# State-space stage: the first pair's read-out taken twice, from the two rotated products

## The chip, the core and the metric

The kernel runs on one core of a Trainium2 chip. The time is the device time of one execution in microseconds. The engines named here are TensorE (matrix products and transposes, into PSUM banks), VectorE and ScalarE (element-wise work), GpSimd, and SyncE, which issues most of the DMA transfers.

## The reference

Two transformer-like blocks of two layers each, on 256 tokens of width 1024. The change lies in one mixer of the second block, a diagonal state-space layer in 64 groups of 16 channels with 64 complex states each. Cut to what matters:

```python
def s5_mixer(h, lam, log_dt, b, c, d_skip, w_glu):
    a_bar = exp(lam * dt)                       # complex, one per group and state
    bu = einsum('gpi,lbgi->lbgp', b_bar, u)     # inputs into the states
    hs = scan: hs[t] = a_bar * hs[t-1] + bu[t]  # complex recurrence over 256 steps
    y = einsum('gop,lbgp->lbgo', cmat, hs).real # read-out
    y = y + d_skip * u
    g = gelu(y)
    val, gate = split(g @ w_glu)
    return val * sigmoid(gate)
```

After it come the residual sum and an MLP of width 4096 with squared ReLU.

## The kernel before

**How it is staged.** The kernel is one hand-ordered program. Each engine has its own instruction list, and semaphores join them; PSUM banks are planned by `Units`. Dense layers run as three products of a high and a low part of weights and activations (L732 to L734); ScalarE makes the high part (L1332) and VectorE the low one (L1723), as weights arrive by DMA into `ring`. The state-space stage lies between the two MLPs, at about 606 to 640 us.

**The state-space stage.** Time is cut into 32 chunks of 8 steps (`L = 8`, `NC = 32`). Inside a chunk the result is a product with precomputed taps (`tap_product`, L1189 to L1199); between chunks a state is carried. The 64 x 64 complex states are in 128 partitions (64 states of two halves, `GH = 2`) times 32 groups. `inject_product` (L1170 to L1178) makes the chunks' inputs to the states in four banks. VectorE turns them with `spin_pair` (L1806 to L1836), once for each pair of banks. It multiplies by cosines and sines of the state's angle (L1815, L1816) into `spun` and `crossed`, sums them into `driven` (L1820, L1821), runs the decay over the chunks with two scans (L1824) into `faded`, turns back with two more products (L1828, L1829), and sums or subtracts these into `states`, shifted by one chunk (L1834), with real and imaginary part side by side. Pair 0 does L1828 to L1834 in one piece of four; pair 1 does it in two.

TensorE then reads out. `read_out` (L1203 to L1216) multiplies each 64 x 32 block of states with 64 x 128 read-out weights into `state_out` banks, adding to what the taps left there. Part 0 uses the states of pair 0, part 1 those of pair 1. Each matrix product in float32 shows as two records. Loop L1235 to L1254 sets TensorE's order: taps of the part, then `keep_busy` (constant products into a bank that nobody reads, counts in `KEEP`, L46), then a wait for `states_ready`, then the read-out; part 1 waits twice, once for each half of its states. `weights_here` waits for the read-out's weights, which SyncE brings in four pieces a part (L670).

**Behind it.** ScalarE copies the `state_out` banks 0, 1 and 3 (L1628) and VectorE bank 2 (L2339, behind one low part of weights, L1723). TensorE transposes (`state_turn`, L1225), ScalarE applies the gelu (L1635 to L1645), and the gated linear unit's products (L732) follow.

**Storage.** `states` is `aux[:, 0:2048]`, pair 0 in its first half. `xg_at` holds the regrouped inputs of the chunks until TensorE has transposed them, and shares its place with `hT_hi`.

The program puts VectorE's order in the stage as: scale three chunk banks (L1804), clear the first column of `states` (L2334), `spin_pair(0)` with the fourth chunk bank scaled inside it after the first injection bank, `spin_pair(1)`, one low part of weights, the copy of bank 2.

## Time and profile before

| | us |
|---|---|
| median of 3 runs | 870.33 (870.22 to 870.56) |
| profiled execution | 871.13 |
| its span in the trace | 869.3 |
| TensorE busy | 852.5 (98%) |
| VectorE busy | 592.2 (68%) |
| ScalarE busy | 442.0 (51%) |
| mean granted clock of TensorE | 0.999 |

In the rows PE is TensorE, PEld its weight loads, DVE VectorE, ACT ScalarE, SP SyncE (SPq its queue of transfers). `L1828` is a line of the kernel. `out<-in` are the kernel's names of buffers, `x12` a count. In a timeline the first number is the start and the second the duration, and `[1.75 <-DVE aux L1834]` says that the engine stood idle for 1.75 us before, until that instruction released it. Matrix products overlap, so the start of the next group tells the pace better than a group's end.

### The profile page before, as it was taken

Reading aid. Unit: us, or ns where it says so; the run is one execution under the profiler, and the core shown is the slowest. Engines: PE = TensorE matmul, PEld = TensorE weight load, DVE = VectorE, ACT = ScalarE, POOL = GpSimd, SP = SyncE. Lnnn points to the kernel's source line nnn. Section 1 sums busy time; section 2 is a strip of 40 time slices with the busy share of each in tenths; the row PEclk is TensorE's granted clock in tenths of the full one; section 3 lists DMA queues with packets and bytes.
Section 4 is the critical chain, followed back from the end, with each engine's and each line's share of the span. In section 5 each row is a group of like instructions: output and inputs, shape, how many; then the busy total and the mean of one; then the engine's idle time right before and its main releaser. Section 6 shows DMA issues by size and latency. Waiting matters only on the chain.

```text
span 869.3 us, 13478 instructions
## 1 busy us (share of the span) xinstructions
PE 852.5 (98%) x5659; PEld 736.7 (85%) x5659; DVE 592.2 (68%) x738; ACT 442.0 (51%) x591; POOL 117.3 (13%) x74
## 2 busy tenths in 40 slices
PE   8999999999999999999999999999989999999998
PEld 7787888888788887888988889997868999999996
DVE  5694577756756678888798788786975655555553
ACT  5644465656954555753553436443254644444450
POOL 1000001111000004114054344440000000000000
PEclk9999999999999999999999999999999999999999
DMA  9936645555004537226455565556966465555521
GB/s 327 335 113 242 242 146 193 194 179 175 35 4 154 177 97 243 97 85 210 167 189 172 209 230 192 209 188 144 287 251 237 152 212 182 186 188 193 194 98 48
DMA packets 68117, 155.96 MB, mean 179 GB/s; under 512 B 3113, under 2 KB 6922, under 8 KB 68058
## 3 DMA queue, kind: packets, MB, share of 16 engines
q1 hardware_dynamic: 65024, 146.80, 50.0%
q0 software_dynamic: 2224, 7.67, 2.6%
q10 hardware_dynamic: 810, 0.63, 0.5%
q8 instruction: 45, 0.74, 0.3%
q14 instruction: 14, 0.11, 0.0%
HBM read 146.70 MB, written 7.34 MB: 177 GB/s over the span
## 4 chain that ended last, share of the span: by engine, by line
PE 88%; DVE 5%; ACT 2%; DMA 2%; SPq 1%; issue 1%; ACTq 0%; DVEq 0%
PE bank L732 18%; PE bank L733 18%; PE bank L734 18%; PE bank L1059 7%; PE bank L1061 7%; PE bank L1057 7%; PE bank L725 3%; DMA ring<-in_a_w_in 2%; PE bank L841 2%; PE bank L831 1%; PE bank L943 1%; PE bank L882 1%; DVE pT L1824 1%; PE bank L1131 1%; DVE wlo L1723 1%
## 5 line engine op out<-in xcount | busy, mean ns | idle before, releaser
L1723 DVE TENSOR_TENSOR wlo<-ring,whi 128x2048 fp32r<-128x2048 f32 (+1 forms) x103 | 251.6, 2449 | 136.8 <-ACT whi L1332 136.4
L1332 ACT ACTIVATE whi<-ring 128x2048 fp32r<-128x2048 f32 (+1 forms) x104 | 198.4, 1909 | 209.2 <-PE bank L734 144.1
L732 PE MATMUL bank<-whi,hT 128*128 128x512 f32 (+1 forms) x512 | 201.8, 394 | 5.3 <-DVE wlo L1952 1.9
L734 PE MATMUL bank<-whi,hT 128*128 128x512 f32 (+1 forms) x512 | 198.8, 388 | 0.0
L733 PE MATMUL bank<-wlo,hT 128*128 128x512 f32 (+1 forms) x512 | 198.7, 388 | 0.0
L1057 PE MATMUL bank<-hT,whi 128*128 128x256 f32 x512 | 145.3, 284 | 0.0
L1059 PE MATMUL bank<-hT,whi 128*128 128x256 f32 x512 | 144.9, 283 | 0.0
L1061 PE MATMUL bank<-hT,wlo 128*128 128x256 f32 x512 | 144.8, 283 | 0.0
L732 PEld LDWEIGHTS bank<-whi,hT 128*128 128x128 f32 x512 | 96.1, 188 | 27.8 <-issue 4.8
L734 PEld LDWEIGHTS bank<-whi,hT 128*128 128x128 f32 x512 | 96.1, 188 | 19.6
L733 PEld LDWEIGHTS bank<-wlo,hT 128*128 128x128 f32 x512 | 96.2, 188 | 18.9 <-issue 0.5
L1057 PEld LDWEIGHTS bank<-hT,whi 128*128 128x128 f32 x512 | 98.2, 192 | 0.6
L1059 PEld LDWEIGHTS bank<-hT,whi 128*128 128x128 f32 x512 | 98.2, 192 | 0.5
L1061 PEld LDWEIGHTS bank<-hT,wlo 128*128 128x128 f32 x512 | 98.2, 192 | 0.0
L732 PE MATMUL bank<-whi,hidT_hi 128*128 128x512 f32 x224 | 88.0, 393 | 0.0
L733 PE MATMUL bank<-wlo,hidT_hi 128*128 128x512 f32 x224 | 87.4, 390 | 0.0
L734 PE MATMUL bank<-whi,hidT_lo 128*128 128x512 f32 x224 | 87.2, 389 | 0.0
L1718 DVE SCALAR_TENSOR_TENSOR wlo<-ring,vcols,whi 128x512 fp32r<-128x512 f32 x64 | 43.8, 746 | 20.5 <-ACT whi L1328 20.5
L1328 ACT ACTIVATE whi<-ring,vcols 128x512 fp32r<-128x512 f32 x64 | 40.9, 711 | 19.2 <-PE bank L734 16.9
L732 PEld LDWEIGHTS bank<-whi,hidT_hi 128*128 128x128 f32 x224 | 42.1, 188 | 9.7 <-issue 1.2
L734 PEld LDWEIGHTS bank<-whi,hidT_lo 128*128 128x128 f32 x224 | 42.1, 188 | 8.9
L733 PEld LDWEIGHTS bank<-wlo,hidT_hi 128*128 128x128 f32 x224 | 42.1, 188 | 8.3
(296 smaller groups left out, 1027.6 us busy)
## 6 DMA issues: line engine op xcount, KB each, us to landing
ring<-in_w_ff SPq DMA_DIRECT2D x64, 1024.0 KB, 5.3
ring<-in_ple_gate_w SPq DMA_DIRECT2D x8, 1024.0 KB, 5.1
ring<-in_w_kv SPq DMA_DIRECT2D x8, 1024.0 KB, 5.0
ring<-in_b_w_in SPq DMA_DIRECT2D x8, 1024.0 KB, 5.0
ring<-in_a_w_in SPq DMA_DIRECT2D x7, 1024.0 KB, 14.5
ring<-in_w_in SPq DMA_DIRECT2D x6, 1024.0 KB, 5.6
ring<-in_w_glu SPq DMA_DIRECT2D x6, 1024.0 KB, 8.9
ring<-in_a_w_out SPq DMA_DIRECT2D x4, 1024.0 KB, 5.6
```

The lines of the kernel that those rows point to most:

```text
L725: last = pe.transpose(b[0:width, cc * S + t * P:cc * S + t * P + P], src[:, t, c * width:(c + 1) * width], ident)
L732: pe.matmul(bank_cols, high[:, at[0], at[1]], w_high, start=first, stop=False)
L733: pe.matmul(bank_cols, high[:, at[0], at[1]], w_low, start=False, stop=False)
L734: return pe.matmul(bank_cols, low[:, at[0], at[1]], w_high, start=False, stop=last)
L841: last = pe.matmul(b[:, :], pT[:, l, k, t * P:(t + 1) * P], ple_rows[:, k, nb * 512:(nb + 1) * 512], start=(k == 0), stop=(k == 1))
L1057: pe.matmul(b[:, at:at + S], w_high[:, kk, cols], hT_hi[:, k, :], start=k == 0 and at == 0, stop=False, skip_group_check=True)
L1059: pe.matmul(b[:, at:at + S], w_high[:, kk, cols], hT_lo[:, k, :], start=False, stop=False, skip_group_check=True)
L1061: last = pe.matmul(b[:, at:at + S], w_low[:, kk, cols], hT_hi[:, k, :], start=False, stop=k == KC - 1, skip_group_check=True)
L1328: ins = act.activation(whi[at][:, n], ring[:, slot[name], cols][:, n], ACT.Copy, scale=gain(gained[name[0]], 4 * (g % 2) + kk))
L1332: act.activation(whi[at], raw_rows(g), ACT.Copy).then_inc(high_made, 1)
L1718: ins = dve.scalar_tensor_tensor(out=wlo[at][:, n], in0=ring[:, slot[name], cols][:, n], scalar=gain(gained[name[0]], 4 * (g % 2) + kk), i ...
L1723: dve.tensor_tensor(wlo[at], raw_rows(g), whi[at], ALU.subtract).then_inc(low_made, 1)
```

## The change

`spin_pair(0)` no longer makes the states of pair 0. It writes the two products of the second turn, the cosine one and the sine one, each in the layout of states and shifted by one chunk, into two buffers `turned[0]` and `turned[1]` (the second with the minus sign folded into its real part), and TensorE reads out both with the same weights into the same banks. The counts of constant products in `KEEP` change from 12 and 5 to 2 and 3. `states_ready` is counted one further. Pair 1 stays.

```diff
--- before.py
+++ after.py
@@ -43,7 +43,7 @@
 LATE_TURN = 1
 REACH = 144
 WARM, HOLD = 9, 5
-KEEP = (0, 3, 12, 5)
+KEEP = (0, 3, 2, 3)
 
 SPLIT = ("u", "za", "a_out", "gate0", "k", "v", "q", "zb", "b_out", "gate1", "wc", "wq", "wk", "wv", "w_o",
          "val", "gate", "f1", "f2")
@@ -562,6 +562,7 @@
         states = aux[:, 0:2048].rearrange("p (x c) -> p x c", c=NC)
         spun, crossed, driven = (aux[:, 2240 + 1024 * n:3264 + 1024 * n].rearrange("p (r m c) -> p r m c", r=2, m=4)
                                  for n in range(3))
+        turned = [v.rearrange("p (x c) -> p x c", c=NC) for v in (aux[:, 0:1024], xg_at[:, 0:1024])]
         faded = pT[:, :, :, :].rearrange("p l k s -> p (l k s)").rearrange("p (r m c) -> p r m c", r=2, m=4)
         waves = h
         fades = sig[:, :, :].rearrange("p b (x c) -> p (b x) c", c=NC)
@@ -1200,6 +1201,21 @@
                                          start=(s == 0), stop=False, skip_group_check=True)
                 last.then_inc(pe_done, 1)
 
+            def read_out_turned(n):
+
+                wr = weights(("readout", 0), 32, P)
+                for half in range(GH):
+                    rows = slice(GP * half, GP * half + GP)
+                    for s in range(4):
+                        for r in range(2):
+                            for q in range(4):
+                                to = slice(32 * QS[q], 32 * QS[q] + 32)
+                                last = pe.matmul(bank(("state_out", half))[to, s * P:(s + 1) * P],
+                                                 turned[n][rows, 16 * r + 4 * q + s, :], wr[rows, 8 * q + 4 * r + s, :],
+                                                 start=False, stop=(n == 1 and r == 1), skip_group_check=True)
+                    if n == 1:
+                        last.then_inc(pe_done, 1)
+
             def read_out(part, halves, quarters):
 
                 wr = weights(("readout", part), 32, P)
@@ -1240,15 +1256,15 @@
                 if part == 0:
                     weights_here(("readout", 0))
                     keep_busy(KEEP[2])
-                    pe.wait_ge(states_ready, 1)
-                    for half in range(GH):
-                        read_out(0, (half,), range(4))
+                    for n in range(2):
+                        pe.wait_ge(states_ready, n + 1)
+                        read_out_turned(n)
                 else:
                     keep_busy(KEEP[3])
-                    pe.wait_ge(states_ready, 2)
+                    pe.wait_ge(states_ready, 3)
                     weights_here(("readout", 1), first=True)
                     read_out(1, (0, 1), (0, 1))
-                    pe.wait_ge(states_ready, 3)
+                    pe.wait_ge(states_ready, 4)
                     weights_here(("readout", 1))
                     read_out(1, (0, 1), (2, 3))
             for n in range(4):
@@ -1816,6 +1832,7 @@
                     dve.tensor_tensor(crossed[:, :, m], b[:, ::-1], both[1][:, :, m], ALU.mult).then_inc(dve_emptied, 1)
                     if pair == odd == 0:
                         scaled_chunks(3)
+                        dve.memset(turned[1][:, :, 0:1], 0.0)
                 dve.wait_ge(dve_emptied, u.emptied(("inject", 2 * pair + 1)))
                 dve.tensor_tensor(driven[:, 0], spun[:, 0], crossed[:, 0], ALU.add)
                 link(dve.tensor_tensor(driven[:, 1], spun[:, 1], crossed[:, 1], ALU.subtract))
@@ -1824,7 +1841,16 @@
                     ins = dve.tensor_tensor_scan(faded[:, r].rearrange("p m c -> p (m c)"), fade,
                                                  driven[:, r].rearrange("p m c -> p (m c)"), 0.0, ALU.mult, ALU.add)
                 link(ins)
-                for m in (slice(0, 2), slice(2, 4)) if pair else (slice(0, 4),):
+                if pair == 0:
+                    one, two = (v.rearrange("p r m (q c) -> p r (m q) c", c=NC)[:, :, :, 0:NC - 1] for v in (faded, faded[:, ::-1]))
+                    cos, sin = (v.rearrange("p r m (q c) -> p r (m q) c", c=NC)[:, :, :, 0:NC - 1] for v in both)
+                    to = [v.rearrange("p (r x) c -> p r x c", r=2)[:, :, :, 1:NC] for v in turned]
+                    dve.tensor_tensor(to[0], one, cos, ALU.mult).then_inc(states_ready, 1)
+                    dve.scalar_tensor_tensor(out=to[1][:, 0], in0=two[:, 0], scalar=-1.0, in1=sin[:, 0], op0=ALU.mult, op1=ALU.mult)
+                    dve.tensor_tensor(to[1][:, 1], two[:, 1], sin[:, 1], ALU.mult).then_inc(states_ready, 1)
+                    dve.wait_ge(states_ready, 2)
+                    return
+                for m in (slice(0, 2), slice(2, 4)):
                     dve.tensor_tensor(spun[:, :, m], faded[:, :, m], both[0][:, :, m], ALU.mult)
                     link(dve.tensor_tensor(crossed[:, :, m], faded[:, ::-1, m], both[1][:, :, m], ALU.mult))
                     for r, op in enumerate((ALU.subtract, ALU.add)):
@@ -1833,7 +1859,7 @@
                         to = states[:, 32 * pair:32 * pair + 32, :].rearrange("p (m r q) c -> p r m q c", m=4, r=2)[:, r, m, :, 1:NC]
                         ins = dve.tensor_tensor(to, one, two, op)
                     ins.then_inc(states_ready, 1)
-                    dve.wait_ge(states_ready, (2 if m.start == 0 else 3) if pair else 1)
+                    dve.wait_ge(states_ready, 3 if m.start == 0 else 4)
 
             def s5_powers():
 
```

## Rows read from the trace of the kernel before

**Rows 1.** The page, parts 1 and 4: busy time, and the chain that ended last.
```profile
PE 852.5 (98%) x5659; PEld 736.7 (85%) x5659; DVE 592.2 (68%) x738; ACT 442.0 (51%) x591; POOL 117.3 (13%) x74
...
PE 88%; DVE 5%; ACT 2%; DMA 2%; SPq 1%; issue 1%; ACTq 0%; DVEq 0%
```

**Rows 2.** Stretches: length, busy of PE, PEld, DVE, ACT, POOL; clock, DMA share, GB/s.
```profile
609.80:614.50 4.70, 4.70 (x142) 4.49 (x142) 3.04 (x7) 0.72 (x1) 0.00 (x0) 1.00 1.04 271
614.50:618.20 3.70, 3.70 (x126) 3.67 (x122) 3.63 (x5) 0.00 (x0) 0.00 (x0) 1.00 0.88 221
...
620.20:623.20 3.00, 2.95 (x13) 2.11 (x12) 2.93 (x5) 0.00 (x0) 0.00 (x0) 1.00 1.03 330
...
629.80:631.50 1.70, 0.00 (x0) 0.00 (x0) 1.65 (x4) 0.86 (x1) 0.00 (x0) 1.00 0.78 270
...
700.00:869.30 169.30, 165.47 (x1037) 150.00 (x1035) 85.93 (x62) 67.86 (x58) 0.00 (x0) 1.00 0.47 158
```

**Rows 3.** Timeline of TensorE through both read-outs, 620 to 636 us.
```profile
620.14 3.01 PE L1232 MATMUL bank<-hT 128*128 128x512 f32 x12
623.22 3.31 PE L1212 MATMUL bank<-ring,aux 64*32 64x128 f32 x128
626.46 1.96 PE L1198 MATMUL bank<-spare,work 128*32 128x128 f32 x64
628.34 1.45 PE L1232 MATMUL bank<-hT 128*128 128x512 f32 x5
631.54 1.95 PE L1212 MATMUL bank<-ring,aux 64*32 64x128 f32 x64 [1.75 <-DVE aux L1834]
633.64 1.95 PE L1212 MATMUL bank<-ring,aux 64*32 64x128 f32 x64 [0.15 <-DVE aux L1834]
```

**Rows 4.** Chain that ended last, 614 to 637 us: start, us, what.
```profile
614.48 0.69 DVE aux L1815
...
633.62 2.29 DVE wlo L1723
...
636.66 0.64 PE bank L1225 x4
```

**Rows 5.** Timeline of VectorE, 610 to 631 us.
```profile
610.83 0.11 DVE L2334 MEMSET aux<- 128x64 f32 x1
...
614.48 0.69 DVE L1815 TENSOR_TENSOR aux<-bank,h 128x512 f32<-128x512 f32 x1 [0.69 <-PE bank L1177]
...
619.51 1.23 DVE L1828 TENSOR_TENSOR aux<-pT,h 128x1024 f32<-128x1024 f32 x1
620.65 1.22 DVE L1829 TENSOR_TENSOR aux<-pT,h 128x1024 f32<-128x1024 f32 x1
621.90 0.67 DVE L1834 TENSOR_TENSOR aux<-aux 128x496 f32<-128x496 f32 x1
...
622.49 0.67 DVE L1834 TENSOR_TENSOR aux<-aux 128x496 f32<-128x496 f32 x1
623.19 0.69 DVE L1815 TENSOR_TENSOR aux<-bank,h 128x512 f32<-128x512 f32 x1
...
630.74 0.74 DVE L1834 TENSOR_TENSOR aux<-aux 128x248 f32<-128x248 f32 x2
```

**Rows 6.** Groups by line and shape on VectorE, whole span: busy, mean ns.
```profile
L1718 DVE SCALAR_TENSOR_TENSOR wlo<-ring,vcols,whi 128x512 fp32r<-128x512 f32 x64 | 43.8, 746 | 20.5 <-ACT whi L1328 20.5
...
L2082 DVE SCALAR_TENSOR_TENSOR aux<-bank,aux 128x384 f32<-128x384 f32 x16 | 8.1, 550 | 3.9 <-ACT aux L1478 3.9
```

**Rows 7.** Timeline of ScalarE: the work that waits behind the copies.
```profile
628.75 1.91 ACT L1332 ACTIVATE whi<-work 128x2048 fp32r<-128x2048 f32 x1 [1.56 <-DMA work<-in_w_glu]
```

**Rows 8.** SyncE's timeline, and the transfer issued last: size, us to landing.
```profile
624.34 2.13 SPq L670 DMA_DIRECT2D ring<-scratch_readout  x2
...
ring<-scratch_readout SPq DMA_DIRECT2D x1, 512.0 KB, 5.7
```

**Rows 9.** Who waited for whom from 640 us on: us, times, longest.
```profile
ACT whi L1332 <- PE bank L734: 57.8, 18, 3.5
```

## The prediction, made before any run of the changed kernel

> **What bounds the kernel now.** I read the page first. TensorE is busy for 98% of the span, and the chain that ended last lies on it for 88% and on VectorE for 5% [rows 1]. The share says only that TensorE is the usual bound; the change sits in a stage where it may not be. So next came the table of stretches from 609.8 us on, to find where TensorE stands still. From 629.80 to 631.50 us it has no work at all while VectorE is busy for 1.65 of 1.70 us, and in the stretches before it VectorE is as busy as TensorE (2.93 of 3.00 us) [rows 2]. TensorE's busy time there is not all useful either: 12 and 5 of its products (L1232) are constant products that `keep_busy` issues to no purpose of the result [rows 3]. The chain of waits settles it: from 614.5 us to the first transpose of the outputs at 636.66 us every piece of it is VectorE's or a hand-over [rows 4]. The timeline of VectorE gives its order and has no hole after the 0.69 us before 614.48 us [rows 5]. The stage is a VectorE chain with TensorE waiting behind it: 1.75 us before the first half of the second read-out (631.54 us), 0.15 us before the other half [rows 3].
>
> So time taken from VectorE between 614.48 and 633.62 us moves the end of the kernel, until something else is late.
>
> **What the change takes from VectorE.** For pair 0, before: two multiplications of 128x1024 (L1828, L1829) and two sums of 128x496 (L1834). They start at 619.51 us, and the next instruction, the first of pair 1, starts at 623.19 us [rows 5]: 3.68 us in all, by start times, which count overlaps and waits once.
>
> After: one multiplication of 2x16x31 = 992 elements a partition, one scalar_tensor_tensor of 496 (the sign of the sine product is folded into it) and one multiplication of 496.
> - The first: L1828 at 1024 elements lasts 1.23 us and its follower starts 1.14 us after it [rows 5]. From this L1828 to the two L1834 of 496 elements, 528 elements are worth 1.23 - 0.67 = 0.56 us, so 32 fewer are worth 0.03: 1.11 us.
> - The scalar_tensor_tensor: no row has it with this shape from the chip's own memory with a constant scalar. With a constant scalar, L2082 takes 550 ns at 384 elements; 112 more at the same slope are 0.12 us, so 0.67 us, what a 496-element sum takes. With a scalar read from memory, L1718 takes 746 ns at 512, so 0.73 at 496 [rows 6]. A follower starts about 0.08 us before the end in the first case (L1834: 621.90 to 622.49 is 0.59 us for a duration of 0.67 [rows 5]). So it is worth 0.59 to 0.65 us; I take 0.60, since the scalar here is a constant, as in L2082.
> - The last: 496 elements with the wait behind it, as the second L1834 from 622.49 to 623.19 us: 0.70 us [rows 5].
>
> Sum 1.11 + 0.60 + 0.70 = 2.41 us, against 3.68: **1.27 us less**, bounds 1.22 to 1.28. None of the access patterns is new: the 31-of-32 step stands in L1834, the exchanged halves and the repeated factors in L1828 and L1829, at the price of plain ones. For patterns merged in a new way I keep 0.1 us on either side.
>
> The added memset of 32 elements costs at most the 0.11 us of the one of 64 (L2334) [rows 5]. It stands behind the scaling of the last chunk bank, before the wait for the second injection bank, where VectorE is idle for 0.69 us before 614.48 [rows 5]: nothing. Behind it are the four injection multiplications of this bank; were the cover gone it would cost its 0.11 us. TensorE waits for the scaling, not for the memset.
>
> The Trainium skill has a rule that could be held against counting by instructions rather than elements ("VectorE: DVE Perf Modes", § The DRAIN you can't avoid): the next operation does not start before the pipe of the last one is empty. Here L1829 starts 1.14 us after L1828, which lasts 1.23 [rows 5], so start times are the better count. By full durations the sum would be 1.19 + 0.67 + 0.67 = 2.53 against 1.23 + 1.22 + 0.67 + 0.67 = 3.79, a gain of 1.26: the same.
>
> **What it adds to TensorE.** Before, the first read-out is 64 products in the program (128 records, since each float32 product shows twice) from 623.22 to the next group's start at 626.46: 3.24 us [rows 3]. After, it is taken twice: 6.48 us. Removed are 10 of the 12 and 2 of the 5 constant products. Twelve take 3.01 us with the last one's tail of about 0.4, so 0.23 each at start: 12 x 0.23 = 2.8 us is the pace, 10 of them 2.3 us, 2 more 0.46 us. TensorE thus gets 3.24 - 2.8 = 0.5 us more work, but it may start earlier: the first copy needs only the cosine product. Working forward:
> - taps end and the constant products start at 620.14; two of them: 620.60
> - cosine product ready at 619.51 + 1.2 = 620.7; with the 0.05 us from VectorE's end to TensorE's start, the read-out starts at 620.75
> - first copy to 623.99, second copy to 627.23. The second one's wait, for a product ready at 619.51 + 2.41 = 621.9, is long over
> - taps of the second part, 626.46 to 628.34 before [rows 3], so 1.88 us: to 629.11
> - three constant products, 0.7 us: 629.8
> - the first half of pair 1's states is ready at 631.5 - 1.27 = 630.2 (the sums of L1834 start at 630.74 and last 0.74 [rows 5]), so TensorE starts at 630.3
> - it takes 1.95 us with its tail [rows 3], to 632.2; the other half is ready at 633.6 - 1.27 = 632.3.
>
> So TensorE is ready 0.5 us before VectorE, where it was 1.75 before. **VectorE still sets the end of the stage**, and TensorE's 0.5 us more is hidden by that wait.
>
> Who else is moved? On TensorE's queue, behind the longer read-out, stand the taps of the second part, covered as worked out. ScalarE copies the first two outputs when they are done. It stands idle for 1.56 us before 628.75, where its next work waits for a transfer [rows 7]: the second copy ended at 627.19. It moves by the 0.77 us by which the read-out ends later (627.23 for 626.46), to 628.0, and still hides. No DMA is added or moved past another. The one transfer that comes close is the last piece of the second read-out's weights: SyncE issues the pair from 624.34 to 626.47 us, and the last takes 5.7 us [rows 8], so it lands at about 631.9 at the latest. TensorE wanted it at 633.64 and will want it at 632.3: 0.4 us to spare.
>
> **After the stage** the subtraction on VectorE (L1723, 633.62 [rows 4]), the copy, the transposes and the gelus follow one on another and start 1.27 us earlier as one. Then TensorE is busy for 165.47 of 169.30 us from 700 us on [rows 2], and from 640 us on the rounding of the weights on ScalarE (L1332) waits for TensorE 18 times, 57.8 us in all [rows 9], never long for a transfer: the weights are there early. Nothing there eats the gain.
>
> The profiled execution took 871.13 us (span 869.3, 1.8 around it), 0.8 above the median of 870.33. The sum is made against its own times: 871.13 - 1.27 = 869.86. The difference carries over: 870.33 - 1.27 = **869.1 us**, by the bounds and 0.1 for the patterns 868.9 to 869.3; 0.2 more on either side for hand-overs that settle otherwise gives 868.7 to 869.5. I call 0.2% (1.74 us) about what a measurement of this kernel can tell from no change; the gain is 0.15%.
>
> **The rivals.**
> (a) *TensorE becomes the bound.* Its margin is only 0.5 us. For: 32 products of the read-out show as 1.95 us a group in part 1, against 3.24/2 = 1.62 by pace in part 0 [rows 3]. If the four groups cost 1.95 each, they take 7.8 us, TensorE is ready at 631.1 instead of 629.8, 0.8 behind VectorE, and the second half starts at about 633.0: 0.7 of the gain is lost, 869.8 us. Against: 1.95 holds a tail that the next product would overlap, and the new loop walks one half at a time exactly as part 0's did. The Trainium skill ("TensorE: Matmul & The Clock Gate", § The mechanism of packing small matmuls) says that a weight load overlaps running matmuls only if it goes to other rows of the array. By that rule the new loop, which stays in one half of the rows, would be the bad order and part 1's, which changes halves, the good one. The rows say otherwise: 1.62 us a group for the bad order, 1.95 at most for the good one [rows 3].
> (b) *The clock falls, and the kernel is slower.* Constant products at full width are cut from 12 to 2 ahead of the read-out, and with them what keeps the array full. The granted clock is 1.00 in every stretch, the 2.4 GHz level [rows 2]. If it went to 1.2 GHz from the second copy (624.0 us) to the transposes, every TensorE piece doubles: +3.24 for the copy, +1.88 for the taps, +0.7 for the constant products, less 0.5 of margin, then +1.7 for each half of the second read-out: 5.3 + 3.4 = 8.7 us, 877.8 us. It decides once the loss passes 1.27 us of gain and 0.5 of margin, that is, from some 3.5 us of work at the lower level. Against: from 609.80 to 618.20 TensorE ran almost only narrow products (64 columns of weights) for over 8 us at 1.00 [rows 2], and the empty 1.7 us at 629.80 is nearly gone after.
> The same page (§ What's actually happening) says the clock is granted by how busy the engine has lately been; by that the changed kernel, with fewer holes, has nothing to fear, and the trace agrees as far as 1.00 goes.
> (c) *The last weights are late.* If its 0.4 us to spare is gone and the piece lands at 633.0 or later, the gain falls to 0.6 or less: 869.8 to 870.3 us. The row is one transfer in a full queue, and no row shows how such a one varies from run to run.
> (d) *More than the sum.* If VectorE's new products cost less than their elements say, or the gelu's hand-overs fall better, 0.5 us more: below 868.6.
>
> **How the numbers follow.** Forecast 0.70, (a) 0.12, (b) 0.06, (c) 0.06, (d) 0.06. Faster by over 0.2% is below 868.59 us: (d), 0.06. Slower by over 0.2% is above 872.07: (b), 0.06. The rest is within: 0.88. The range takes in the forecast and nearly all of (a) and (c): 868.6 to 870.3; it leaves out (b), (d) and the tails of (c), some 0.14.
>
> **What would show it.** Right: in the changed kernel the first instruction of pair 1 (L1815's kind) starts about 2.4 us after the scans end and not 3.7; the read-out of the first part stands as two runs of 3.2 us without a hole; TensorE waits for VectorE about 0.5 us before the next read-out; the first transposes start near 635.4 us; the clock stays 1.00. Wrong: a wait of VectorE's for nothing between scans and pair 1, TensorE without a wait at 630 us (then (a)), a wait for the weights of L670 (then (c)), a clock below 1.00 (then (b)), or a hole of over 0.3 us after 640 us that was not there before.

## The result: slower, because TensorE ran out of instructions and then lost its clock

| | us |
|---|---|
| kernel before, median of 11 executions | 870.52 (870.18 to 870.75) |
| changed kernel, median of 11 executions | 874.68 (870.31 to 876.09) |
| ratio, with 95% interval | 1.0043 (1.0034 to 1.0051) |
| profiled execution of the changed kernel, and its span | 872.81, 871.0 |

Forecast was 869.1 us, 868.6 to 870.3. The kernel is 4.2 us slower instead of 1.4 faster. Its executions also spread over 5.8 us where the old one's spread over 0.6; in the sessions of the experiments the old kernel itself spread over 1.6 to 3.4 us. The granted clock, a mean over the whole execution, is 0.993 to 0.998 in ten of them; the eleventh, the fastest at 870.31 us, has 0.999. The profiled execution, 872.81 us, is the second fastest of the eleven.

VectorE's timeline in the changed kernel (start, duration, line) answers to [rows 5]:

```profile
612.92 0.09 DVE L1835 MEMSET xg_at<- 128x32 f32 x1
613.63 0.69 DVE L1831 TENSOR_TENSOR aux<-bank,h 128x512 f32<-128x512 f32 x1 [0.62 <-PE bank L1178]
...
618.66 1.19 DVE L1848 TENSOR_TENSOR aux<-pT,h 128x992 f32<-128x992 f32 x1
619.77 0.67 DVE L1849 SCALAR_TENSOR_TENSOR xg_at<-pT,h 128x496 f32<-128x496 f32 x1
620.35 0.67 DVE L1850 TENSOR_TENSOR xg_at<-pT,h 128x496 f32<-128x496 f32 x1
621.05 0.69 DVE L1831 TENSOR_TENSOR aux<-bank,h 128x512 f32<-128x512 f32 x1
...
637.56 0.69 DVE L2365 COPY work<-bank 128x512 f32<-128x512 f32 x1 [3.30 <-PE bank L1228]
```

The new products take 2.39 us from 618.66 to 621.05; the sum said 2.41. The memset hides before the wait. But at the end of the stage VectorE now waits 3.30 us for TensorE. TensorE's timeline answers to [rows 3]:

```profile
619.20 0.73 PE L1248 MATMUL bank<-hT 128*128 128x512 f32 x2
619.90 3.30 PE L1213 MATMUL bank<-ring,aux 64*32 64x128 f32 x127
624.03 0.29 PE L1213 MATMUL bank<-ring,aux 64*32 64x128 f32 x1 [0.83 <-issue]
624.04 3.30 PE L1213 MATMUL bank<-ring,xg_at 64*32 64x128 f32 x127
629.13 0.29 PE L1213 MATMUL bank<-ring,xg_at 64*32 64x128 f32 x1 [1.79 <-issue]
629.37 3.51 PE L1199 MATMUL bank<-spare,work 128*32 128x128 f32 x64
632.81 1.03 PE L1248 MATMUL bank<-hT 128*128 128x512 f32 x3
633.77 3.76 PE L1228 MATMUL bank<-ring,aux 64*32 64x128 f32 x128
638.40 1.94 PE L1241 MATMUL bank<-cst,work 128*128 128x128 f32 x16 [0.86 <-DVE work L2365]
```

Two things are new. Before the last record of each copy of the read-out (a float32 product shows as two records) TensorE stands still for 0.83 and 1.79 us, and the reason is "issue": no wait that the profile shows. And behind the second hole the taps take 3.44 us to the next start where they took 1.88 [rows 3]. The table of stretches says why:

```profile
623.20:626.40 3.20, 2.37 (x102) 2.37 (x105) 3.13 (x5) 0.34 (x1) 0.00 (x0) 1.00 1.03 395
626.40:629.80 3.40, 1.61 (x48) 1.22 (x44) 3.30 (x6) 0.59 (x2) 0.00 (x0) 0.97 0.93 334
629.80:631.50 1.70, 1.70 (x40) 1.70 (x36) 1.62 (x4) 1.70 (x2) 0.00 (x0) 0.50 0.68 199
631.50:635.60 4.10, 4.10 (x97) 3.28 (x91) 2.29 (x1) 0.36 (x1) 0.00 (x0) 0.82 1.04 382
```

The clock (third number from the end) is 0.50, the 1.2 GHz level, where TensorE was empty before the change [rows 2]. In the chain that ended last VectorE's share falls from 5% [rows 1] to 3%:

```profile
PE 90%; DVE 3%; ACT 2%; DMA 2%; SPq 1%; issue 1%; ACTq 0%; DVEq 0%
```

**The account of this execution.** This stage began 0.85 us earlier than before, at 608.95 for the first injection product against 609.80 (the work ahead of it is the same; over all traces of this case the stage begins between 608.75 and 611.72 us), so all is counted from there. By the forecast the transposes should start at 636.66 - 0.85 - 1.27 = 634.54 us; they start at 638.40, 3.86 late. The start of the read-out, 619.90, is the forecast one. From there to the taps it took 9.47 us instead of 6.48, +2.99: the holes, 2.62, and about 0.2 after each until the products overlap again. Taps +1.56, constant products +0.26: 4.81 us, less the 0.5 of margin, so the second read-out starts 4.3 us late, at 633.77 for 629.45. It takes 3.76 us where the forecast had 3.95 with a wait for VectorE in it, and the hand-over behind it takes 0.86 for 1.07, since VectorE's weights no longer stand right before the copy: 3.9 us.

Against the kernel before, the stage of this execution is 2.6 us longer (29.45 us from the first injection product to the first transpose, for 26.86). The medians differ by 4.2 us. The other 1.6 us belong to slower executions of which there is no trace; nine of them are slower than this one, seven with a mean clock of 0.993 to 0.996 against 0.998 here. More time at the lower clock or longer holes would both explain them; neither is shown.

### The profile page after: what moved, and what is told of

It is laid out like the page before. It is cut to its first block, busy times and chain, and to the rows that moved or that the text cites. A ratio compares the mean times of both kernels' runs of the same rounds, so it can differ in the third digit from the quotient of the medians.

```text
span 871.0 us, 13710 instructions
## 1 busy us (share of the span) xinstructions
PE 854.7 (98%) x5775; PEld 739.5 (85%) x5775; DVE 590.8 (68%) x738; ACT 441.7 (51%) x591; POOL 117.2 (13%) x74
## 4 chain that ended last, share of the span: by engine, by line
PE 90%; DVE 3%; ACT 2%; DMA 2%; SPq 1%; issue 1%; ACTq 0%; DVEq 0%
PE bank L733 18%; PE bank L735 18%; PE bank L734 18%; PE bank L1060 7%; PE bank L1062 7%; PE bank L1058 7%; PE bank L726 3%; DMA ring<-in_a_w_in 2%; PE bank L842 2%; PE bank L1178 1%; PE bank L832 1%; PE bank L1213 1%; PE bank L1199 1%; PE bank L944 1%; PE bank L883 1%
```

## What the experiments asked

The holes are 128 records apart, each with a weight load of its own: 256 instructions. The page of the changed kernel counts its transfers of instructions:

```profile
q8 instruction: 46, 0.75, 0.4%
```

That is 16 KB each, over 13710 instructions of all engines. So **theory A**: TensorE's instructions arrive in blocks of 256; a read-out uses a block in 3.24 us [rows 3]; the next is not there in that time, since its transfer shares DMA engines that are full with data (share 1.03 and 0.93 above). The clock falls on top of it.

The Trainium skill ("Runtime: NRT & Kernel Launch", § Instruction fetch mechanics) states the same block, 16 KiB or 256 instructions, and that crossing one is mostly hidden. The trace agrees on the block; here the crossing was not hidden.

**Rival B**: the second copy is simply too much work, or too slow with its new buffers. **Rival C**: the holes alone, or the cut of the constant products alone, bring down the clock.

Where an experiment's time is compared, the median of the kernel before is that of the same chip session: 870.97 us for e1 to e4, 870.57 for e5, e6, e8 and e9, 871.14 for e7, e10 and e11, 870.80 for e12. The runs e3, e6, e7 and e10 leave out part of the result or make it from old data.

The medians hold noise that does not come from this stage. A cleaner measure is the length of the stage in each run's trace, from the first injection product to the first transpose of the outputs. Behind it every trace takes the same 232.6 to 232.8 us to its end. These are single executions:

| run | stage begins | transposes begin | stage, us | against before |
|---|---|---|---|---|
| before | 609.80 | 636.66 | 26.86 | |
| changed | 608.95 | 638.40 | 29.45 | +2.59 |
| e1, constant products back at 12 and 5 | 611.36 | 644.09 | 32.73 | +5.87 |
| e2, six products between the copies | 609.57 | 639.36 | 29.79 | +2.93 |
| e3, VectorE's side alone | 609.08 | 634.66 | 25.58 | -1.28 |
| e4, TensorE's side alone | 609.28 | 643.09 | 33.81 | +6.95 |
| e5, before with 2 and 3 constant products | 609.19 | 636.09 | 26.90 | +0.04 |
| e6, changed with light transfers | 609.60 | 635.30 | 25.70 | -1.16 |
| e7, changed with one light transfer | 609.15 | 637.24 | 28.09 | +1.23 |
| e8, GpSimd makes both sums | 609.42 | 635.00 | 25.58 | -1.28 |
| e9, GpSimd makes one sum | 609.82 | 637.22 | 27.40 | +0.54 |
| e10, before with light transfers | 611.72 | 638.60 | 26.88 | +0.02 |
| e11, e8 with 12 and 5 | 609.89 | 637.04 | 27.15 | +0.29 |
| e12, e8 with 17 and 4 | 608.75 | 634.84 | 26.09 | -0.77 |

The mean clock of a whole execution has to be read with the same care. In the traces of e1 and e10 the clock was also at 0.50 for some 3.4 us from about 35 us on, far ahead of this stage, and e10's mean is 0.998 although its stage ran at 1.00. So a mean of 0.998 alone does not place a fall here.

### e3: VectorE's side alone

```diff
-                    for n in range(2):
-                        pe.wait_ge(states_ready, n + 1)
-                        read_out_turned(n)
+                    pe.wait_ge(states_ready, 1)
+                    read_out_turned(0)
```
and `KEEP = (0, 3, 12, 5)`; the stop flags and the count that frees the banks move to this one copy.

> The changed kernel with the second copy of the read-out left out on TensorE (the sine product is made but never read out, so the first pair's part of the result is incomplete), and the constant products at 12 and 5. VectorE's side of the change stands alone. If the sum of the prediction for VectorE was right and everything lost is lost on TensorE, no hole is left and the time is 869.1 us (1.2 to 1.3 us under the kernel before). If VectorE's new products or what follows them cost more than thought, it is 870.3 us or more.

869.57 us, ratio 0.9988 (0.9979 to 0.9996). TensorE's timeline, from before the taps:

```profile
616.06 2.00 PE L1178 MATMUL bank<-work 128*64 128x32 f32 x62 [0.37 <-issue]
...
619.88 3.35 PE L1247 MATMUL bank<-hT 128*128 128x512 f32 x12
623.15 3.31 PE L1213 MATMUL bank<-ring,aux 64*32 64x128 f32 x128
626.39 1.96 PE L1199 MATMUL bank<-spare,work 128*32 128x128 f32 x64
628.28 1.43 PE L1247 MATMUL bank<-hT 128*128 128x512 f32 x5
629.64 3.96 PE L1227 MATMUL bank<-ring,aux 64*32 64x128 f32 x128
634.66 1.94 PE L1240 MATMUL bank<-cst,work 128*128 128x128 f32 x16 [1.07 <-DVE work L2363]
```

No hole in the read-outs. The gain, 1.4 us by medians and 0.35 to 1.8 by the interval, holds the 1.27 of the sum, and the stage of the trace is 1.28 us shorter. So VectorE's part of the forecast stands, and everything is lost on TensorE. A small hole of 0.37 us stands among the injection products, in e4 too, and in e5 one of 0.65: the shortage can show outside the read-outs.

### e4: TensorE's side alone

```diff
-KEEP = (0, 3, 12, 5)
+KEEP = (0, 3, 2, 3)
...
+                    for half in range(GH):
+                        read_out_idle(half)
                     for half in range(GH):
                         read_out(0, (half,), range(4))
```
`read_out_idle` is the same loop into the banks of the injections, which nobody reads by then.

> The kernel before with VectorE untouched, but with an extra copy of the first read-out on TensorE, into banks nobody reads, ahead of the real one, and the constant products at 2 and 3. TensorE's side of the change stands alone. The copies start at 623.2 instead of 620.7 us, so even without holes TensorE is some 0.8 us late for the second read-out: 871.3 us. Theory A (short of instructions): the same two holes, 256 instructions apart, and the clock falls behind them in most executions: 874 to 878 us. Rival (the holes come from the new buffers, or from the two copies adding into the same banks): no hole, 871.3 us.

876.74 us, ratio 1.0068 (1.0056 to 1.0081), with the old buffers, the old sums and separate banks:

```profile
622.70 3.60 PE L1226 MATMUL bank<-ring,aux 64*32 64x128 f32 x128 [1.84 <-DVE aux L1848]
626.02 3.30 PE L1212 MATMUL bank<-ring,aux 64*32 64x128 f32 x127
633.30 0.42 PE L1212 MATMUL bank<-ring,aux 64*32 64x128 f32 x1 [3.98 <-issue]
633.65 3.64 PE L1198 MATMUL bank<-spare,work 128*32 128x128 f32 x64
```

The hole stands at the same record of the second copy, 3.98 us long. At the first copy's border there is at most 0.3 us (3.60 for 3.30): TensorE had waited 1.84 us for VectorE before it, time in which a block could arrive. The new buffers and the adding into one bank are out. The theory said two holes; there was one large and one nearly closed.

### e6 and e10: fewer bytes in the way

```diff
-                sp.dma_start(val_rows[:, half, :].rearrange("p (k n) -> p k n", k=KC // 2),
+                many = 4 if half else 1
+                sp.dma_start(val_rows[:, half, 0:512 * many].rearrange("p (k n) -> p k n", k=many),
...
-                        sp.dma_start(ring[:, slot[name], at:at + 1024], src).then_inc(block_landed[slot[name]][q % 2], 16)
+                        wide = 128 if name[1] else 1024
+                        sp.dma_start(ring[:, slot[name], at:at + wide], src[:, 0:wide]).then_inc(block_landed[slot[name]][q % 2], 16)
```

> The changed kernel with two groups of transfers made small: the first half of the gated unit's value weights (a quarter of its bytes) and the weights of the second read-out (an eighth), so that part of the result is made from what lay there before. TensorE's and VectorE's lists are untouched. If the holes are instructions that come late because their transfer queues with the data on the DMA engines, they shrink to under half, the clock is 1.00 and the time 869 to 870.5 us. If they have a cause of their own on TensorE, they stay at 0.8 and 1.8 us or more, and the time at about 875 us.

869.72 us, ratio 0.9994 (0.9985 to 1.0002), clock 0.998 to 1.000:

```profile
624.16 0.29 PE L1215 MATMUL bank<-ring,aux 64*32 64x128 f32 x1 [0.27 <-issue]
624.17 3.30 PE L1215 MATMUL bank<-ring,xg_at 64*32 64x128 f32 x127
627.89 0.29 PE L1215 MATMUL bank<-ring,xg_at 64*32 64x128 f32 x1 [0.42 <-issue]
```

With TensorE's and VectorE's lists untouched the holes shrink from 0.83 and 1.79 to 0.27 and 0.42 us, and the median is 5.0 us under the changed kernel's, each in its own session. This is the strongest evidence for theory A: nothing but bytes was taken away. By the queue of instruction transfers, in windows of 0.1 us, the blocks begin to move at 616.5, 621.3, 626.7 and 633.0 us in the changed kernel, 4.8 to 6.3 us apart; with light transfers at 617.7, 621.8 and 625.3, 4.1 and 3.5 apart.

The start of a block and the end of a hole belong together in every trace. There are sixteen holes of 0.25 us or more in this stage with "issue" as the reason, in ten of the runs, and TensorE goes on 2.2 to 2.8 us after a block has begun to move in all of them. What varies is the time before that: from TensorE's going on at such a border to the start of the next block it is 1.2 and 2.1 us in e6 and 1.3 to 6.0 us elsewhere. So of the time that a block takes, the part that gets longer is its wait to be moved.

The control is the kernel before with the same transfers made light:

> The kernel before with the same transfers made small as in e6_light_transfers (same parts of the result left to old data). It is the control: its time says what light transfers give without the change. If instructions are never short in the kernel before, 870.3 to 870.6 us, nothing gained, and the changed kernel's 869.72 us with light transfers is a gain of 0.6 to 0.9 us of the 1.27 that the sum gave. If it drops to about 869.7 too, the change gains nothing even without holes.

870.79 us, ratio 0.9996 (0.9987 to 1.0005): nothing gained that can be measured. So light transfers help the changed kernel alone. What the change is worth in that pair of kernels the times can't tell: by medians about 0.5 us (870.79 - 869.72 = 1.07, of which 0.57 is the difference between the two sessions' kernel before), but the two ratios are 0.9994 and 0.9996 and neither interval excludes 1. The traces say more: the stage is 1.16 us shorter in e6 and as long as before in e10, with 0.7 us of holes left.

### e7: which transfer

Of the edit of e6 only the first part, the value weights.

> The changed kernel with only the first half of the gated unit's value weights made small (a quarter of its bytes; part of the result is made from what lay there before); the second read-out's weights are whole again. It stands in the queue between the pieces of the second read-out, from 622 us on. If this transfer holds up the block of instructions behind the second hole, that hole shrinks to under 1 us and the first (0.8 us, before this transfer is issued) stays: 870.5 to 872 us. If the read-out weights are what holds it up, the hole stays at 1.8 us or more: 874 to 875 us.

873.43 us, ratio 1.0026 (1.0012 to 1.0040). In the profiled execution the holes are 1.05 and 1.52 us. That misses both sides of the expectation, but lies nearer to the second: together the holes are as long as in the changed kernel, 2.57 us for 2.62. By the difference to e6 the read-out's own weights are the larger part of what stands in the way; no run has these alone made light. Of its 12 executions, the five with a clock of 1.000 took 871.8 to 873.7 us; of the seven others, 0.992 to 0.999, one took 879.1.

### e1 and e2: constant products put back, or put between

```diff
-KEEP = (0, 3, 2, 3)
+KEEP = (0, 3, 12, 5)
```

> The changed kernel with the counts of constant products put back from 2 and 3 to 12 and 5, and nothing else. The trace of the changed kernel shows two holes of TensorE without any wait, 0.83 and 1.79 us, 256 instructions apart (issue), and a clock of 0.50 right behind the second. Theory A (TensorE runs out of instructions: they come in blocks, and the products of the read-out use them up faster than they come; the hole then drops the clock, because full-width products no longer surround it): the clock is back at 1.00 or nearly, the constant products stand where TensorE waited for instructions, and the time is 870 to 871.5 us. Theory B (TensorE's added work alone makes it late; the constant products do not matter for the clock): 2.8 us of constant products come on top of a TensorE that is already late, so about 877 us with the clock still at 0.996. Theory C (holes alone drop the clock, whatever stands around them): 874 to 876 us, as the changed kernel.

876.76 us, ratio 1.0067 (1.0053 to 1.0082):

```profile
624.83 2.98 PE L1213 MATMUL bank<-ring,aux 64*32 64x128 f32 x116
...
627.90 2.73 PE L1213 MATMUL bank<-ring,xg_at 64*32 64x128 f32 x105
633.46 1.06 PE L1213 MATMUL bank<-ring,xg_at 64*32 64x128 f32 x11 [2.83 <-issue]
634.45 3.64 PE L1199 MATMUL bank<-spare,work 128*32 128x128 f32 x64
```

Time and clock are those that rival B expected: once TensorE is the bound, constant products cost their full time. The hole B can't explain, and its place speaks for theory A. Ten more constant products ahead of the copies are 20 more instructions, and the hole stands before the eleventh record from the end instead of before the last: ten records with their loads, 20 instructions earlier. The border belongs to the instruction list, not to the work. The first border, now eleven records before the end of the first copy, shows no hole: the constant products put off the copies until 624.83 us, and the block for it began to move at 624.3. The one hole that is left is longer, 2.83 us. The clock falls all the same, to 0.50 from 632.4 us on, still within the hole (in e4 too, at 632.2). So what theory A said of the clock, that full-width products around the hole would hold it, is wrong.

e2 puts six products between the copies:

```diff
                         pe.wait_ge(states_ready, n + 1)
+                        if n:
+                            keep_busy(6)
                         read_out_turned(n)
```

> The changed kernel with 6 constant products (1.4 us at full clock) added between the two copies of the read-out. Theory A (short of instructions): these products take 12 instructions for 1.4 us, so they fill time in which TensorE would have stood still; the second hole shrinks from 1.79 us to about 0.4, TensorE ends the second copy no later than before, the clock stays at 1.00, and the time falls from 874.7 to 870 to 871.5 us. Theory B (TensorE simply has too much work): 1.4 us more, 876 us or more.

875.75 us, ratio 1.0056 (1.0038 to 1.0074). The hole did not shrink, it is 2.20 us long, and it moved seven records earlier for six products and a wait:

```profile
625.16 1.66 PE L1248 MATMUL bank<-hT 128*128 128x512 f32 x6
626.75 3.09 PE L1213 MATMUL bank<-ring,xg_at 64*32 64x128 f32 x120
632.05 0.42 PE L1213 MATMUL bank<-ring,xg_at 64*32 64x128 f32 x8 [2.20 <-issue]
```

The block behind it began to move at 629.7 us, 7.4 after the one before (622.3); in the changed kernel it was 5.4. So a block has no fixed time, and filling time ahead of it did not help. I had taken it as fixed. That it depends on the data in the queues when it is asked for fits e6, but is not shown for this block. The clock stayed at 1.00 in the profiled execution with 3.3 us of holes, so the holes are not an effect of a low clock. The two executions at 1.000 took 873.7 and 873.8 us, the four with a lower mean clock 875.3 to 878.9: without a fall the holes and the added products cost about 3 us against the kernel before, and the executions with a lower clock 1.6 to 5.1 more.

### e5: the constant products alone

The kernel before with `KEEP = (0, 3, 2, 3)`.

> The kernel before with only the counts of constant products changed, from 12 and 5 to 2 and 3. TensorE then waits idle for VectorE from about 620.6 to 623.2 us. If the cut of the constant products alone brings the clock down, the granted clock is under 1.00 in most executions and the time 873 us or more. If it takes the holes of instruction supply as well (theory A), the clock stays at 1.00 and the time is that of the kernel before, 870.3 to 871.2 us; the read-out may even start a block of instructions earlier, but TensorE waits for VectorE anyway.

870.77 us, ratio 1.0006 (0.9997 to 1.0015), but with a clock of 0.993 to 0.998 in all 11 executions. The stretches of the profiled one, with the wait of 1.56 us for VectorE in the first:

```profile
620.20:622.60 2.40, 0.84 (x10) 0.37 (x2) 2.33 (x4) 0.00 (x0) 0.00 (x0) 1.00 1.02 329
622.60:627.46 4.86, 4.86 (x128) 4.47 (x128) 4.79 (x7) 0.60 (x1) 0.00 (x0) 0.65 1.02 365
627.46:631.90 4.44, 4.44 (x71) 3.44 (x67) 4.33 (x8) 2.51 (x2) 0.00 (x0) 0.61 0.92 333
```

In the kernel before's own 33 executions of that session the mean clock is 0.998 in three and 0.999 or 1.000 in the others. The cut of the constant products is enough to lose the clock, without a second copy and without a hole in the read-outs; the hole of 0.65 us among the injections ended at 616.45 us, 7.7 us before the fall, and e3 kept 1.00 with one of 0.37 there. The time hardly shows the fall. The read-out takes 4.85 us instead of 3.24 and the taps 3.55 instead of 1.88, but behind them stood the 1.75 us in which TensorE waited for VectorE [rows 3], and the second read-out then passes in one piece of 3.31 us where its two halves with their wait took 4.05. The expectation that tied a falling clock to 873 us or more had forgotten that cover. The changed kernel has used it up.

### e8, e9, e11, e12: the same relief without TensorE

If the fault is instructions, VectorE should be relieved by an engine that isn't TensorE. GpSimd is idle here and takes over the sums of pair 0, with 17 and 3 constant products (`state_sum` is the sum of L1834 as a function of the engine):

```diff
+            pool.wait_ge(turns_made, 1)
+            for r in range(2):
+                ins = state_sum(pool, 0, r, slice(0, 4), *first_turns)
+            ins.then_inc(sums_made, 1)
...
+                if pair == 0:
+                    dve.tensor_tensor(first_turns[0], faded, both[0], ALU.mult)
+                    ins = dve.tensor_tensor(first_turns[1], faded[:, ::-1], both[1], ALU.mult)
+                    ins.then_inc(turns_made, 1)
+                    dve.wait_ge(turns_made, 1)
+                    return
```

> The kernel before with the same 1.27 us taken from VectorE in another way that adds no instruction to TensorE: GpSimd, idle here, makes the two sums of the first pair's states (from products in a buffer of their own), VectorE goes straight on to pair 1, and the constant products are 17 and 3. GpSimd took 3.0 us for 1152 elements in this kernel, so 2.6 us for 992: the first read-out starts at 624.6 instead of 623.2 us, its end and the taps of part 1 at 629.7, and the states of part 1 are ready at 630.3. If nothing but instruction supply spoiled the change, no hole appears and the time is 1.0 to 1.3 us below the kernel before, 869.2 to 870.0 us. If VectorE is slowed while GpSimd works (its L1723 took 2.63 instead of 2.29 us on average near GpSimd's work), some 0.4 us of it are lost; if GpSimd takes over 3.5 us, TensorE is late and the gain is gone.

869.88 us against 870.57, but the ratio is 0.9997 (0.9989 to 1.0006). The mechanism works: GpSimd takes 2.48 us for both, VectorE goes on at once and keeps its pace, TensorE has no hole in this execution:

```profile
621.58 2.48 POOL L574 TENSOR_TENSOR aux<-xg_at 128x496 f32<-128x496 f32 x2 [16.25 <-DVE xg_at L1839]
```
```profile
624.11 3.31 PE L1222 MATMUL bank<-ring,aux 64*32 64x128 f32 x128 [0.39 <-POOL aux L574]
...
635.00 1.94 PE L1235 MATMUL bank<-cst,work 128*128 128x128 f32 x16 [1.07 <-DVE work L2355]
```

The stage of this execution is 1.28 us shorter, all of VectorE's gain, but the executions run from 868.95 to 872.40 us. With one of the two sums on GpSimd (e9, `KEEP` 13 and 4) there are holes again:

> As e8_gpsimd_sums, but GpSimd makes one of the two sums and VectorE the other; constant products 13 and 4. VectorE is 0.6 us shorter instead of 1.27, and the first read-out waits for GpSimd only until about 623.4 us. If instruction supply and GpSimd's speed both leave room: 0.5 to 0.6 us below the kernel before. If GpSimd's time is the problem of e8, this one is the better of the two.

870.43 us, ratio 0.9997 (0.9984 to 1.0009), 0.65 and 1.57 us of holes in the profiled execution:

```profile
634.15 2.20 PE L1222 MATMUL bank<-ring,aux 64*32 64x128 f32 x82 [1.57 <-issue]
```

e11 leaves the counts at 12 and 5, e12 takes 17 and 4:

> The kernel of e8_gpsimd_sums with the constant products left at 12 and 5. TensorE has an empty 1.5 us before the first read-out (622.6 to 624.1) and is ready for the second one 0.4 us after VectorE's states instead of 0.1. If only VectorE's time counts: 0.3 us over e8, 870.2 us. If the clock needs the constant products right up to the read-out, it falls in some executions and the time spreads to 872 us and more.

> The kernel of e8_gpsimd_sums with 17 and 4 constant products instead of 17 and 3, to see whether this way to relieve VectorE beats the kernel before by more than the measurement's spread. The fourth product of the second group costs 0.23 us of TensorE's time, in which it is ready about 0.1 us after VectorE's states. If the gain of VectorE's 1.27 us holds: 869.7 to 870.2 us, 0.5 us or more below the kernel before measured beside it. If late instructions eat it in some executions, as in the kernel with one sum on GpSimd, the executions spread up to 872 us and the gain is not measurable.

e11: 870.77 us, ratio 0.9989 (0.9978 to 1.0000), spread 868.87 to 872.76, three of 12 executions at clock 0.996 and 872.6 to 872.8 us. e12: 870.28 us, ratio 0.9999 (0.9988 to 1.0010), spread 869.29 to 874.23. All medians lie 0.1 to 0.7 us under the kernel before, and no interval excludes no change. The traces of e8 and e12 show that 1.28 and 0.77 us can be had in the stage. Those of e9 and e11 show them lost, to the holes above and in e11 to one of 0.25 us and a wait of 0.60 for the read-out's weights. How often each happens no run tells, and part of the spread is noise that the old kernel has as well. None of the four is shown to beat the kernel before.

## Why the prediction was wrong, point by point

**VectorE's sum: right.** 2.39 us in the changed kernel and 2.40 in e3, forecast 2.41. Small terms too: the scalar_tensor_tensor is worth 0.58 us by start times, I took 0.60; the memset 0.09, hidden.

**Working forward on TensorE: the step that failed.** "First copy to 623.99, second copy to 627.23": the start was right, and so was the pace while there were instructions (127 records in 3.30 us with the tail, as 128 in 3.31 before [rows 3]). What was wrong is that a pace read from one group of 3.24 us [rows 3] was laid twice end to end. The group before it is 12 constant products, 24 instructions in 2.8 us; two copies are 512 instructions in 6.5. In the old program blocks of instructions began to move at 617.3, 622.5 and 628.6 us, 5.2 and 6.1 apart, and none was late; the new one uses a block up in 3.2 us while they begin to move 4.8 to 6.3 apart. The two copies measured 9.47 us instead of 6.48. Nothing in my sum counted instructions per microsecond, though the page lists their transfers and [rows 2] shows the DMA engines at 0.9 to 1.0.

**"TensorE gets 0.5 us more work": misleading.** It is right in time of products, and hides that 24 instructions (12 products with their weight loads) were exchanged for 256.

**Rival (a)**, TensorE becomes the bound, happened, but by holes and not by a slower pace, and at 3.0 us instead of the 1.3 that it priced; so its 869.8 us was far too low.

**Rival (b)**, the clock falls, happened too and was given 0.06. The argument against it, that narrow products had run for 8 us at 1.00, was a bad neighbour: e5 shows a fall with the fewer constant products and no second copy. Its price was fair in kind (taps 3.44 us for 1.88, as doubled) and too long in reach: in the profiled execution the clock is back at 1.00 by the second read-out. The sentence from the Trainium skill that the clock follows how busy the engine was ("TensorE: Matmul & The Clock Gate", § What's actually happening) I read as speaking for the change, as it would have fewer holes. The trace agrees as far as the changed kernel had more holes, not fewer, and its clock fell 0.5 us behind the longer one. But e2 kept 1.00 in its trace with longer holes and e5 fell with none in the read-outs, so how long TensorE stood still does not by itself tell the clock here.

**Rival (c)**, late weights, did not happen here. It did in e11, where TensorE waited 0.60 us for them before the last half. **(d)** did not.

**Behind the stage** nothing ate anything, as said: from 700 us on TensorE is busy for 167.15 of 171.00 us, and from the first transpose to the end it is 232.6 us in both kernels.

**What stays open.** Why blocks begin to move 3.5 us apart once and 7.4 another time: e6 and e7 together say that the read-out's weights count for more than the value weights, not by what rule. And what exactly drops the clock: e5 fell with a wait of 1.56 us and no hole in the read-outs, e1 with 17 constant products and a hole of 2.83, while e2's profiled execution kept 1.00 with holes of 1.11 and 2.20. So a fall came with a hole while 12 and 5 constant products were in place (e1), and with fewer of them while the read-outs had no hole (e5): both halves of rival C stand, but neither is a rule. There is no profile of an execution at or above the median (874.68 us) of the changed kernel.

## What to carry to other kernels

Before moving work to TensorE as many small products, count its instructions per microsecond, weight loads and the two passes of float32 included, and set them against the DMA load of the same stretch. Here some 80 per us (256 in 3.24 us) was too much beside full DMA engines, and about 45 (256 in 5.2 to 6.1 us) was not; the injection products, 65 per us, stood in between, with a hole in three of the traces and none in the others. Constant products that help to keep the clock also thin out the instruction list; exchanging them for dense work of the same length gives up both. And where a wait is removed, ask what it was covering: in e5 it covered a slow clock, in e4 the arrival of a block. Last, when the gain is as small as the noise of the whole kernel, compare the length of the stage in the traces too.

## What the runs showed of the hardware that I had not expected

- TensorE stops without any wait at borders 256 instructions apart when small products run densely beside full DMA engines: 0.25 to 3.98 us at the borders where it stopped. It went on 2.2 to 2.8 us after the next block had begun to move (sixteen holes in ten runs). The border moves with the instruction list (20 instructions in e1).
- Cutting bytes from unrelated transfers shrinks these holes (1.79 to 0.42 us in e6).
- With 2 and 3 instead of 12 and 5 constant products the mean clock was 0.993 to 0.998 in 11 of 11 executions (e5), at a cost in time of 0.2 us, within what can't be measured: a lower clock alone need not show in the time.
- The clock fell while TensorE stood still in e1 and e4 (0.50 from 632.4 and 632.2 us), 0.5 us after it went on in the changed kernel, and not at all in e2 with holes of 1.11 and 2.20 us.
- GpSimd's two sums of 496 elements took 2.48 us, and VectorE's products beside them kept their 0.60 us from start to start.
